# State updates of the samples by rounded halves on all rows of the array, and their numerators with the queries as weights, in four column groups

## The reference

```python
# mlstm_scan, one chunk
num = einsum('btsh,bshv->bthv', qk, vc) + w_inter[..., None] * einsum('bthk,bhkv->bthv', qc, C)
C_new = sc_prev[..., None, None] * C + einsum('bsh,bshk,bshv->bhkv', sc, kc, vc)
# gla_scan, one chunk
o = einsum('btsh,bshv->bthv', att, vc) + einsum('bthk,bhkv->bthv', qc * exp(b), S)
S_new = exp(bL)[..., None] * S + einsum('bshk,bshv->bhkv', kc * exp(bL[:, None] - b), vc)
```

## Time and profile before

| | |
|---|---|
| Time, median of three runs | 2382.94 us (2374.94 to 2383.36) |
| The profiled execution: its own time, its span | 2379.16 us, 2377.4 us |
| TensorE, matmuls busy | 98% of the span |
| VectorE, ScalarE, GpSimd busy | 45%, 28%, 1% |
| Weight products of 288 columns (L436) and 256 columns (L646) | 82% and 3% of the chain that ended last |
| L531, L688 and L535 in that chain | 1%, 1% and under 1% |
| Mean granted clock of TensorE | 0.989 |

### The profile page before, as it was taken

How to read it: one execution, slowest core, us unless ns; L and a number is a source line. 1 busy time by engine, 2 the same in 40 slices (tenths; PEclk the granted TensorE clock), 3 DMA queues, 4 the chain that set the end, 5 groups by cost and what they waited for, 6 DMA issues and landing times.

```text
span 2377.4 us, 39495 instructions
## 1 busy us (share of the span) xinstructions
PE 2340.4 (98%) x17304; PEld 2308.7 (97%) x17304; DVE 1079.6 (45%) x1395; ACT 666.0 (28%) x806; POOL 29.7 (1%) x20
## 2 busy tenths in 40 slices
PE   7999999999999999999999999999999999999997
PEld 7999999999999999999999999999989899999997
DVE  5334334684545433324553343353754454334245
ACT  4212222453423222212332121244221332122122
POOL 0000000000000000000000000000000100000000
PEclk9999999999989999999999999999998999999999
DMA  4222222232322222222322222222122222222221
GB/s 173 88 89 71 89 79 63 89 115 88 112 88 79 89 88 72 88 89 62 98 80 81 88 73 86 80 80 89 54 74 74 93 72 88 89 81 79 89 68 61
DMA packets 72552, 201.29 MB, mean 85 GB/s; under 512 B 7268, under 2 KB 26980, under 8 KB 72448
## 3 DMA queue, kind: packets, MB, share of 16 engines
q1 hardware_dynamic: 72448, 199.80, 26.0%
HBM read 187.82 MB, written 11.95 MB: 84 GB/s over the span
## 4 chain that ended last, share of the span: by engine, by line
PE 91%; DVE 4%; issue 3%; ACT 1%; POOL 0%; DMA 0%; DVEq 0%; SPq 0%; POOLq 0%; ACTq 0%
PE ps L436 82%; PE ps L646 3%; PE ps L531 1%; PE ps L516 1%; PE ps L688 1%; DVE w_lo L1472 1%; PE ps L666 1%; DVE og L1639 0%; PE ps L677 0%; PE ps L695 0%; PE ps L680 0%; PE ps L535 0%; DVE x L2123 0%; PE ps L487 0%; POOL scratch L1452 0%
## 5 line engine op out<-in xcount | busy, mean ns | idle before, releaser
L436 PE MATMUL ps<-xn_hi,w_hi 128*128 128x288 f32 x3328 | 721.2, 298 | 12.8 <-DVE w_lo L1472 11.5
L436 PE MATMUL ps<-xn_hi,w_lo 128*128 128x288 f32 x3328 | 714.3, 296 | 0.0
L436 PE MATMUL ps<-xn_lo,w_hi 128*128 128x288 f32 x3328 | 714.1, 296 | 0.0
L436 PEld LDWEIGHTS ps<-xn_hi,w_hi 128*128 128x128 f32 x3328 | 537.4, 189 | 17.4 <-DVE w_lo L1472 11.5
L436 PEld LDWEIGHTS ps<-xn_hi,w_lo 128*128 128x128 f32 x3328 | 537.9, 189 | 0.0
L436 PEld LDWEIGHTS ps<-xn_lo,w_hi 128*128 128x128 f32 x3328 | 537.8, 189 | 0.0
L1074 ACT ACTIVATE w_hi<-raw 128x1024 fp32r<-128x1024 f32 x332 | 331.3, 1046 | 361.3 <-PE ps L436 327.4
L1472 DVE TENSOR_TENSOR w_lo<-raw,w_hi 128x1024 fp32r<-128x1024 f32 x332 | 393.4, 1226 | 40.4 <-ACT w_hi L1074 38.3
L436 PE MATMUL ps<-h_lo,w_hi 128*128 128x288 f32 x1616 | 352.2, 297 | 2.6 <-DVE h_hi L1785 2.6
L436 PE MATMUL ps<-h_hi,w_hi 128*128 128x288 f32 x1616 | 352.0, 297 | 1.4 <-DVE w_lo L1472 1.4
L1517 DVE TENSOR_TENSOR scratch<-ps,rstd 128x576 f32<-128x576 f32 x88 | 66.7, 758 | 537.0 <-PE ps L436 533.9
(11 more groups left out here) (229 smaller groups left out, 1590.8 us busy)
## 6 DMA issues: line engine op xcount, KB each, us to landing
raw<-in_w_gate SPq DMA_DIRECT2D x88, 512.0 KB, 3.3
raw<-in_w_up SPq DMA_DIRECT2D x88, 512.0 KB, 4.4
raw<-in_w_down SPq DMA_DIRECT2D x64, 512.0 KB, 3.7
raw<-in_w_mix SPq DMA_DIRECT2D x64, 512.0 KB, 4.2
raw<-in_w_down SPq DMA_DIRECT2D x32, 384.0 KB, 3.7
state_s<-in_state_c SPq DMA_DIRECT2D x4, 1024.0 KB, 7.1
out_c_s<-state_s SPq DMA_DIRECT2D x4, 1024.0 KB, 4.5
state_s<-in_state_g SPq DMA_DIRECT2D x4, 1024.0 KB, 6.7
```

Of the source, the lines that this page charges most:

```text
L436: ins = nc.tensor.matmul(o, a, b[:, c] if c is not None else b, start=first and j == 0, stop=last and j == 2)
```

## The change

**State updates.** Keys and values are split into rounded halves. ScalarE writes `vs_hi`, the rounded values, twice, on partitions 0 to 63 and 64 to 127. GpSimd makes `vs_lo` = values - `vs_hi` on 64 partitions, and `k_hl`, the rounded keys on partitions 0 to 63 and their rest on 64 to 127, and masks it to `k_tok_b` of 128 partitions. A sample's update is then one fp32r product over 128 rows ((k_high + k_low) x v_high) and one over 64 rows (k_high x v_low).

**Numerators.** `sample_stage`, in the first piece, takes the queries as weights: for j = 0 to 3, 32 query columns (16 tokens of two samples, the other 16 unused) by the two states of these samples, 512 moving columns, into PSUM partitions 32j to 32j + 31, so each product uses its own 32 columns of the array. ScalarE copies the bank to SBUF (`take_stage`). `sample_numerator`, in the last piece, waits for this copy, and per half a multiplies values by scores and adds the staged block, turned by products with columns of the identity (two of 32 moving columns).

Three small constants' tiles move to a shared region to make room for `late_stage`. The lists of VectorE and SyncE are the same instructions as before; ScalarE has three more a head.

```diff
@@ PE
-            def sample_piece(mixer, h, bank, i, n):
-
-                a, per = 2 * i // n, 2 * DEC_BATCH // n
...
-                    nc.tensor.matmul(ps[:, bank, a * SAMPLE + b * DEC_SEQ:a * SAMPLE + (b + 1) * DEC_SEQ],
-                                     state_s[:, b, ds], qt[:, h, ts],
-                                     start=b == 0, stop=True, skip_group_check=True)
...
+            def sample_stage(mixer, h, bank):
+
+                for j in range(4):
+                    ins = nc.tensor.matmul(ps[32 * j:32 * (j + 1), bank, :], qt[:, h, 16 * j:16 * j + 32],
+                                           state_s[:, 2 * j:2 * j + 2, :], start=True, stop=True)
+                ins.then_inc(stage_done, 1)
+
+            def sample_numerator(mixer, h, bank):
+
+                pe.wait_ge(stage_taken, N_HEADS * mixer + h + 1)
+                for a in range(2):
+                    vs = slice(h * DV + a * P, h * DV + (a + 1) * P)
+                    out = ps[:, bank, a * SAMPLE:(a + 1) * SAMPLE]
+                    nc.tensor.matmul(out, v_tok[0:SAMPLE, 0, vs], att(mixer, h)[0:SAMPLE, SEQ:TOK],
+                                     start=True, stop=True, skip_group_check=True)
+                    for i in range(2):
+                        ins = nc.tensor.matmul(out.rearrange("p (j r) -> p j r", r=16)[:, :, 8 * i:8 * i + 8],
+                                               staged(mixer)[:, i, a * P:(a + 1) * P],
+                                               ident.rearrange("p (j r) -> p j r", r=32)[:, :, 8 * i:8 * i + 8],
+                                               start=False, stop=True, skip_group_check=True)
+                if mixer == 1:
+                    ins.then_inc(num_s_done, 1)
...
+                    if i == 0:
+                        sample_stage(mixer, h, bank)
+                    elif i == n - 1:
+                        sample_numerator(mixer, h, bank)
...
             def sample_updates(h, part, bank):
 
                 for b in range(4 * part, 4 * part + 4):
-                    ins = nc.tensor.matmul(ps[:, bank + (b % 4) // 2, (b % 2) * DV:(b % 2 + 1) * DV],
-                                           k_tok_b[:, b, :], v_tok[0:SAMPLE, 0, h * DV:(h + 1) * DV],
-                                           start=True, stop=True)
+                    out = ps[:, bank + (b % 4) // 2, (b % 2) * DV:(b % 2 + 1) * DV]
+                    nc.tensor.matmul(out, k_tok_b[:, b, :], vs_hi[:, :], start=True, stop=False)
+                    ins = nc.tensor.matmul(out, k_tok_b[0:SAMPLE, b, :], vs_lo[:, :], start=False, stop=True)
                 ins.then_inc(us_half, 1)
...
@@ ScalarE
+            def take_stage(mixer, h, bank):
+
+                u = N_HEADS * mixer + h
+                act.wait_ge(stage_done, u + 1)
+                nc.scalar.activation(staged(mixer), ps[:, bank, :].rearrange("p (i n) -> p i n", n=DV), ACT.Copy)\
+                    .then_inc(stage_taken, 1)
...
+            def high_values(mixer, h):
+
+                u = N_HEADS * mixer + h
+                act.wait_ge(mx_free, MX_V[mixer][h])
+                if u:
+                    act.wait_ge(us_half, 2 * u)
+                    act.wait_ge(vs_lo_done, u)
+                for r in (0, SAMPLE):
+                    nc.scalar.activation(vs_hi[r:r + SAMPLE, :], v_tok[0:SAMPLE, 0, h * DV:(h + 1) * DV], ACT.Copy)\
+                        .then_inc(vs_hi_done, 1)
...
@@ GpSimd
             for u in range(2 * N_HEADS):
 
+                hs = slice(u % N_HEADS * DV, (u % N_HEADS + 1) * DV)
+                pool.wait_ge(vs_hi_done, 2 * u + 2)
+                G.tensor_tensor(vs_lo[:, :], v_tok[0:SAMPLE, 0, hs], vs_hi[0:SAMPLE, :].bitcast(f32), ALU.subtract)\
+                    .then_inc(vs_lo_done, 1)
                 pool.wait_ge(ktok_ready, u + 1)
+                G.tensor_copy(k_hl[0:SAMPLE, :], k_tok_s[:, :]).then_inc(pool_chain, 1)
+                pool.wait_ge(pool_chain, 2 * u + 1)
+                G.tensor_tensor(k_hl[SAMPLE:P, :], k_tok_s[:, :], k_hl[0:SAMPLE, :].bitcast(f32), ALU.subtract)\
+                    .then_inc(pool_chain, 1)
...
-                nc.gpsimd.tensor_tensor(k_tok_b[:, :, :], bcast_mid(k_tok_s[:, :], DEC_BATCH), bcast(batch, DK),
-                                        ALU.mult).then_inc(keys_b_done, 1)
+                G.tensor_tensor(k_tok_b[:, :, :], bcast_mid(k_hl[:, :].bitcast(f32), DEC_BATCH), bcast(batch2, DK),
+                                ALU.mult).then_inc(keys_b_done, 1)
```

More of the change, by code:

```diff
@@ L160, in program @@
         k_tok_s = sb("k_tok_s", [SAMPLE, DK])
-        k_tok_b = sb("k_tok_b", [SAMPLE, DEC_BATCH, DK])
+        k_hl = sb("k_hl", [P, DK], f32r)
+        k_tok_b = sb("k_tok_b", [P, DEC_BATCH, DK], f32r)
+        vs_hi, vs_lo = sb("vs_hi", [P, DV], f32r), sb("vs_lo", [SAMPLE, DV], f32r)
         ps = ctx.enter_context(nc.psum_tensor("ps", [P, 8, 512], f32))
@@ L179, in cut2, with staged @@
             return ap.rearrange("p (c n) -> p c n", c=2)
+        def staged(mixer):
+            return late_stage[:, :, :] if mixer else T(4)[:, 0:2 * DV].rearrange("p (i n) -> p i n", n=DV)
         def bcast(ap, n):
@@ L274, in program @@
         mx_done, mx_free, rt_done, rt_taken = (sem(n) for n in ("mx_done", "mx_free", "rt_done", "rt_taken"))
-        keys_b_done, hsq_sum = sem("keys_b_done"), sem("hsq_sum")
+        keys_b_done, hsq_sum, vs_hi_done, vs_lo_done, pool_chain = (
+            sem(n) for n in ("keys_b_done", "hsq_sum", "vs_hi_done", "vs_lo_done", "pool_chain"))
+        stage_done, stage_taken = sem("stage_done"), sem("stage_taken")
         num_s_done, ht_s_ready, hsq_s_done, us_half, st_half = (sem(n) for n in (
@@ L541, in early_gates, with sample_pieces, at @@
+            def sample_pieces(mixer, h, bank):
+                def at(i, n):
+                    if i == 0:
+                        sample_stage(mixer, h, bank)
+                    elif i == n - 1:
+                        sample_numerator(mixer, h, bank)
+                return at
             def early_gates(mixer, base):
@@ L757, in sample_part @@
                     pe.wait_ge(state_in, 16 * (h + 1))
-                    return lambda i, n: sample_piece(0, h, 7, i, n)
+                    return sample_pieces(0, h, 7)
                 def sample_den(h):
@@ L886, in sample_part @@
                         pe.wait_ge(hvar_ready, N_HEADS + h)
-                    return lambda i, n: sample_piece(1, h, bank, i, n)
+                    return sample_pieces(1, h, bank)
                 def sample_updates_of(h, part, bank):
@@ L1266, in mlstm_mix @@
                 gate_block(0, 0, mx_free, MX_O[0][0])
+                high_values(0, 0)
                 exponentials(1)
                 for h in range(1, N_HEADS):
+                    if h > 1:
+                        take_stage(0, h - 1, 7)
                     second_gate(h - 1)
@@ L1284, in mlstm_mix @@
                     gate_block(0, 2 * h, mx_free, MX_O[0][h])
+                    high_values(0, h)
                     if h < 3:
                         exponentials(h + 1)
+                take_stage(0, 3, 7)
                 second_gate(3)
@@ L1345, in gla_mix @@
                 split_at(2)
+                high_values(1, 0)
                 for h in range(2):
@@ L1355, in gla_mix @@
                     high(1, h)
+                    high_values(1, h + 1)
                 split_at(7)
+                take_stage(1, 2, 7)
                 sample_squares(1, 2, 7)
@@ L1362, in gla_mix @@
                 high(1, 2)
+                high_values(1, 3)
                 gate_block(1, 6, mx_free, MX_O[1][3])
+                take_stage(1, 3, 7)
                 gate_block(1, 7, psum_free, base + O_AT[1][3] + 1)
```

20 lines of the change are left out of this document (15 added, 5 removed).

## The result

The change makes the kernel a little faster: the median of eight runs is 2364.55 us (2364.15 to 2365.96), against 2379.22 us (2374.94 to 2393.25) for eight runs of the kernel before. The ratio is 0.9935, with a 95% interval of 0.9917 to 0.9953. The forecast was 2379 us; the time is that of rival (a), 2366 us. The profiled execution took 2364.19 us, with a span of 2361.9 us, 15.5 us shorter than before.

What follows compares the result with a forecast made beforehand. TensorE, with matmuls under way for 98% of the span, was taken to bound the kernel. 2379.2 + 5.0 (updates) - 0.2 (numerators) - 7 (clock) = 2377, plus 2 for the median: 2379 us, range 2364 to 2398.

Steps and rivals of the forecast that it cites:

- rival (a): Numerators' four 32-column products run beside each other in both passes; 2366 us, chance 0.23.
- The first part: Numerators' four fp32 queries-by-states products per head, claimed to overlap only partly: 2.18 us a head, 17.4 in all.
- T: Time of one of the two matmuls of an fp32 product with 512 moving columns: 0.43 us.
- about 1: Sign of being wrong: us from the first 32-column matmul to the next weight product, instead of 1.2, 2.5 or 3.8.
- the numerators: Net change of TensorE's steps for both new numerator parts against the old ones: -0.2 us (serial +10.2, beside each other -10.6).
- the three terms: The summed changes over the kernel: state updates +5.0 us, numerators -0.2 us, clock -7 us.
- hi to lo: State updates: step from a high product on 128 rows to the low one on 64, claimed 0.307 us.
- The updates' steps: State updates: twelve lone halves cost +4.1 us, two pairs at the mixers' ends 0.45 each; +5.0 us.
- The second part: Numerators' scores products and turned staged block in the last piece: 2.52 us per mLSTM head, 1.85 per GLA, 17.5 in all.
- The added waits: TensorE's waits on ScalarE's stage copy and GpSimd's keys, claimed covered: cost 0; uncovered copy about 1 us a head.
- The clock: Half-clock stretches at the heads' numerators, blamed on 8-column matmuls; half of 14 us won back: -7 us, bounds 0 and -14.
- the 2 us laid on: Added to the forecast sum because the profiled execution was 3.8 us under the median of three.

Runs made afterwards that it cites:

- e4: Changed kernel with the four 32-column products on only two column groups, in the order 0, 0, 1, 1; 2374.17 us (one run).
- e3: Changed kernel with all four 32-column products sent to the same 32 columns of the array; 2388.12 us (one run).
- e2: Kernel before with only the new numerators, state updates still plain fp32 on 64 rows; 2356.14 us, ratio 0.9902.
- e1: Kernel before with only the new state updates, numerators as before; 2380.86 us, ratio 0.9989.
- e9: Kernel before with each state-by-query product (L531) streaming all 64 query columns instead of 8, numerators wrong in value; 2364.74 us, ratio 0.9935.
- e6: Changed kernel with the low products of the state updates also on all 128 rows, so no shape changes there; 2336.66 us, ratio 0.9809.

## Why the prediction was wrong

**The step that failed** is "The first part": "matmuls start in order, and the two of one product need the same columns, so only the second of one and the first of the next overlap: 5T = 2.18, 17.4". The first part is 2T a head, not 5T: 1.00 us from the first 32-column matmul to the next weight product, which the prediction itself named as a sign of being wrong ("about 1"). Order holds only inside a group of columns: after and e4 show it in their starts, e3 shows the price of sharing (3.55 against 1.00 us a head). Taken at 2T, the forecast's own sum gives -10.6 for the numerators, and e2 has -10.9; the rows of before could not show it, since none has two groups. The forecast had the three terms at -2.2 together; the steps and the clock of all runs make -17.0. The numerators account for 10.7 of the difference, the clock for 2.8 and the updates for 1.6. Here the Trainium skill was right and the reading of the trace too cautious: by its rule (TensorE: Matmul & The Clock Gate, "Part 3: Packing small matmuls") matmuls in different groups run at once, a few ns apart, and the trace has 7 ns. What becomes of the second pass of an fp32 product stood open; that both passes run beside those of the other groups, after and e4 show.

**What held.** T is 0.43 and the changes of shape cost what was worked out (hi to lo 0.31). The updates' steps were forecast at +5.0 and are 3.4 by e1's runs and 5.6 by its rows: the lone halves grow by 0.39 instead of 0.34, and the pairs at the mixers' ends by 0.47, for which 0.45 was forecast, for the reason given: y's low part comes behind the first half's states. The second part was forecast at 2.52 for a head with denominators, and is 2.62. The added waits cost nothing: the stage copy of head 0 runs from 545.05 to 545.64 (forecast: "near 545.6"), though L547 stands at 546.29 and not after 547, so the margin was 0.65 us. GpSimd's products on 128 partitions took 1.90 us in six of the eight heads, the lower bound of 1.9 to 3.8, but 4.81 and 3.66 in the first two of GLA; TensorE waited for none.

**The clock** was forecast at -7 and gave -9.1 between the profiled executions, -9.8 over all runs. The suspicion on the 8-column matmuls was right, and e9 shows it; to take half back was too little, since e9 had 16 us and e2 0.9950 for 0.9877, 15 us. Whether the updates cost some of the clock beside the new numerators (0.9930 for e2's 0.9950) is not shown: the two were not timed side by side, and before's own clock moves as much between chips. What was missed in method is that a span without its clock says little here: 7 us of forecast clock and 7 of steps are each less than the 21 us over which the spans before spread.

**The chances.** 0.23 for rival (a) was low for the one case that a stated rule supported, against an argument from starts in rows in which all matmuls share columns. The sum of (a), 2366, is 1.5 us off, and that closeness is in part luck. With the steps as measured and without the 2 us laid on (the median of eight runs, 2379.22, is the profiled execution's 2379.16) it would say 2362, below the result, whose medians lie 2.3 us closer together than the mean spans.

## What to carry to other kernels

Small products that go to different groups of 32 columns cost as much as the longest queue of one group, both fp32 passes included, so spread them evenly; the order 0, 0, 1, 1 of e4 did no harm. What they and others pay for is each change of the used rows or columns, 0.2 us: sort by shape, or pad with rows that are computed anyway, before saving streamed columns. And where TensorE is called busy but its matmuls stream few columns, look at the granted clock, of every run: in e9 wider moving operands at the pace of the weight loads were free and won it back.

## What the runs showed of the hardware that was not expected

- The start order across column groups is not the program's: 13 ns between products 0 and 2 in e4, with product 1 0.88 us later, if the two passes of a product follow each other there as in the earlier trace rows (else 0.45).
- A product over 64 rows between products over 128 rows takes 0.31 us instead of 0.12 and streams the same; without these changes of shape the kernel is 20.4 us shorter in its steps (e6).
- 64 moving columns instead of 8 cost nothing in steps (-0.8 us for 256 matmuls), and raised the mean clock by 0.008, 16 us.
- GpSimd took 1.90 us for 128 x 1024 in six heads of eight, and 1.89 for 64 x 1024 before (L1448 in the earlier trace rows) in five: that time did not follow the partitions. The other heads took 3.66 and 4.81 us after, and 2.43 to 3.13 before; why stays open. One of each kind, after:

```profile
1705.53 4.81 POOL L1517 TENSOR_TENSOR k_tok_b<-k_hl,cst 128x1024 fp32r<-128x1024 f32 x1
...
1813.08 1.90 POOL L1517 TENSOR_TENSOR k_tok_b<-k_hl,cst 128x1024 fp32r<-128x1024 f32 x1
```

- The runs of the kernel before differ by up to 21 us in span, and the mean granted clock of a run (0.983 to 0.993) tells it with a standard deviation of 0.9 us. After, with the thin matmuls gone, all eight runs have 0.993 and lie within 1.8 us.
